# Attention's eight blocks of queries in another order, beside a recurrence

## The reference, cut to what matters

```
for blk in range(S // Q_BLOCK):              # 8 blocks, 8 heads
    q0 = blk * Q_BLOCK; kend = q0 + Q_BLOCK
    s = einsum('bqhd,bkhd->bhqk', q[:, q0:kend], k[:, :kend]) * scale
    s = where(mask, s, -1e30)
    prob = softmax(s)
    outs.append(einsum('bhqk,bkhd->bqhd', prob, v[:, :kend]))
return concatenate(outs).reshape(B, S, 512) @ w_o_mla
...
state = state * d_t + sa[..., None] * b_t + v_t[..., None] * k_t   # per token
y_t   = einsum('bhvk,bhk->bhv', state, r_t)
```

## Time and profile before

| | us |
|---|---|
| median of three runs | 2992.31 |
| the profiled execution | 2994.15 |
| its span, first to last instruction | 2992.1 |
| stage of the attention with the recurrence | 1681 to 1977 |

### The profile page before, as it was taken

The page is one execution under the profiler, slowest core; times in us unless marked ns, Lnnn a source line. Parts: engine busy times, 40 slices in busy tenths (PEclk is TensorE's granted clock), DMA queues, the critical chain, the costliest instruction groups (busy, mean ns, idle before and its releaser), DMA issues.

```text
span 2992.1 us, 37222 instructions
## 1 busy us (share of the span) xinstructions
PE 2851.3 (95%) x15872; PEld 2312.5 (77%) x15872; DVE 1393.9 (47%) x1950; ACT 758.8 (25%) x1027; POOL 362.6 (12%) x286
## 2 busy tenths in 40 slices
PE   5879999999999999999898989889999999999998
PEld 4767878888888888877777667668888888888876
DVE  6994433332323355545544656645343333334454
ACT  4134311111111231124443443332211111111232
POOL 0000201010000101000001602203211110111221
PEclk9999999999999999999999989989999999999999
DMA  3142111111111113334547124343111111111111
GB/s 141 53 82 91 51 57 43 57 42 46 53 42 57 43 46 122 118 137 134 160 152 193 55 58 143 114 148 134 43 43 57 43 57 42 57 43 46 53 57 57
DMA packets 222627, 236.86 MB, mean 79 GB/s; under 512 B 60448, under 2 KB 175008, under 8 KB 221568
## 3 DMA queue, kind: packets, MB, share of 16 engines
q1 hardware_dynamic: 222464, 234.50, 24.5%
HBM read 178.50 MB, written 56.20 MB: 78 GB/s over the span
## 4 chain that ended last, share of the span: by engine, by line
PE 81%; DVE 11%; ACT 3%; issue 2%; SPq 2%; DMA 1%; POOL 1%; DVEq 0%; ACTq 0%; POOLq 0%
PE bank L630 21%; PE bank L632 21%; PE bank L631 21%; PE bank L1812 1%; PE bank L2495 1%; PE bank L1814 1%; PE bank L1813 1%; PE bank L3259 1%; PE bank L3261 1%; PE bank L2750 1%; PE bank L3260 1%; PE bank L3268 1%; DVE stat L2621 1%; DVE w_lo L183 1%; DVE tmp L183 1%
## 5 line engine op out<-in xcount | busy, mean ns | idle before, releaser
L630 PE MATMUL bank<-op_hi,w_hi 128*128 128x512 f32 x1824 | 712.2, 390 | 1.7 <-DVE gates L672 1.5
L632 PE MATMUL bank<-op_hi,w_lo 128*128 128x512 f32 x1824 | 710.5, 390 | 0.0
L631 PE MATMUL bank<-op_lo,w_hi 128*128 128x512 f32 x1824 | 710.4, 389 | 0.0
L630 PEld LDWEIGHTS bank<-op_hi,w_hi 128*128 128x128 f32 x1824 | 343.0, 188 | 74.1 <-issue 2.9
L632 PEld LDWEIGHTS bank<-op_hi,w_lo 128*128 128x128 f32 x1824 | 342.9, 188 | 71.7
L631 PEld LDWEIGHTS bank<-op_lo,w_hi 128*128 128x128 f32 x1824 | 343.0, 188 | 70.9
L183 DVE TENSOR_TENSOR w_lo<-w_raw,w_hi 128x2048 fp32r<-128x2048 f32 (+3 forms) x119 | 256.9, 2159 | 209.3 <-ACT w_hi L432 205.1
L630 PE MATMUL bank<-f_hi,w_hi 128*128 128x512 f32 x864 | 337.4, 391 | 3.2 <-POOL f_lo L183 3.2
L631 PE MATMUL bank<-f_lo,w_hi 128*128 128x512 f32 x864 | 337.3, 390 | 0.0
L632 PE MATMUL bank<-f_hi,w_lo 128*128 128x512 f32 x864 | 337.1, 390 | 0.0
L183 DVE TENSOR_TENSOR hT<-hT,bank 128x512 f32<-128x512 f32 x256 | 169.8, 686 | 316.5 <-PE bank L632 316.2
(11 more groups left out here) (464 smaller groups left out, 3829.9 us busy)
## 6 DMA issues: line engine op xcount, KB each, us to landing
record<-record_scratch SPq DMA_DIRECT2D x16, 1024.0 KB, 5.3
w_raw<-in_w_ffn_up SPq DMA_DIRECT2D x16, 1024.0 KB, 5.1
w_raw<-in_w_ffn_down SPq DMA_DIRECT2D x16, 1024.0 KB, 4.9
w_raw<-in_w_in SPq DMA_DIRECT2D x13, 1024.0 KB, 5.8
w_raw<-in_w_gate SPq DMA_DIRECT2D x11, 1024.0 KB, 5.1
w_raw<-in_w_up SPq DMA_DIRECT2D x11, 1024.0 KB, 5.1
w_raw<-in_w_down SPq DMA_DIRECT2D x10, 1024.0 KB, 4.9
w_raw<-in_w_in SPq DMA_DIRECT2D x17, 512.0 KB, 4.6
```

Of the source, the lines that this page charges most:

```text
L630: t.matmul(ps[:], hi[:, k, wc], x[0][:, k, xc], start=n == 0, stop=False)
L631: t.matmul(ps[:], hi[:, k, wc], x[1][:, (k + turn) % KD, xc], start=False, stop=False)
L632: last = t.matmul(ps[:], lo[:, k, wc], x[0][:, k, xc], start=False, stop=n == kt - 1)
```

## The change

The order of the blocks becomes 6, 5, 4, 1, 2, 3, 0, 7. SPLIT_FIRST becomes 6, so that o is split for the first seven blocks together, which in this order are the columns 0 to 895, in four chunks in steps 60 to 63; w_o's quarters follow in steps 64 to 67; block 7's columns come last, at step 68. The recurrence keeps its steps.

```diff
-    blocks = tuple(reversed(range(SJ)))
+
+    blocks = (6, 5, 4, 1, 2, 3, 0, 7)
     units = [(i, h) for i in blocks for h in range(NH)]
...
-    SPLIT_FIRST = 5
+    SPLIT_FIRST = 6
...
             if done == SPLIT_FIRST and left < 4:
-                split(done, slice(blocks[done] * P, L), left)
+                split(done, slice(0, SPLIT_FIRST * P + P), left)
             elif SPLIT_FIRST < done < SJ and left == 0:
                 split(done, slice(blocks[done] * P, (blocks[done] + 1) * P), slice(0, 4))
             elif done == SPLIT_FIRST and left >= 4:
```

## The result

The changed kernel takes 3003.95 us in the median of seven runs, against 2992.58 for the kernel before in its seven; the ratio is 1.0031, 95% interval 1.0019 to 1.0043, so 9 us slower, between 5.7 and 12.9. The profiled execution took 3006.75 us; its span, 3005.0 us, is 12.9 us longer than that of before. 2.9 us of this lie before the attention's first softmax, in code that did not change (its start is 1689.38 in place of 1686.53), and -0.4 behind the stage; the stage itself, from the first softmax to the first output matmul, is 10.4 us longer.

The account below looks back on a forecast made before the run. TensorE bounds most of the attention stage, its end being loosest; -2.0 - 2.7 - 9.3 + 18.9 + 1.8 = +6.7 us gives a median of 2999.0 us, own range 2994 to 3003, stated range 2988.5 to 3007.

Parts of the forecast that it names:

- rival 2: Block 7 at the end: clock falls to half for 20.3 us, +9 for +1.8, total 3006 us; chance 0.15.
- Solving: Units 0 to 11: VectorE's reduction of scores shrinks 0.13 us in each of 11 units; -2.0 us (-1.0 to -3.2).
- Gap: Units 12 to 16: smaller by 0.44 us each, but the 24.5 us transfer stays, so TensorE waits longer; 0.
- Ends: Units 17 to 21: TensorE-bound, each loses one block of keys; -2.7 us (-1.5 to -3.5).
- Scan: Units 22 to 47: block 1 replaces block 4, less 2.2 us for norms and shorter cover; -9.3 us (-12 to -5).
- The end: Unit 48's softmax to first output matmul: blocks 0 and 7 there take 56.7 us, not 37.8; +18.9 (+11.5 to +24).
- The loop of the split: Units 60 to 62: ScalarE and VectorE alternate on o's split before the next maximum; 5.4 us each, above TensorE's 4.0.
- Clock: Inside block 7 at the end: one short fall, 3.7 us at half clock; +1.8 us (0 to +9).
- The sign that would have made the forecast wrong: Units 48 to 63: clock staying 1.0 there; other signs were an end under 50 us, scan gain under 5 us.
- the rule named beside this term: Trainium skill: many small gaps between matmul groups can make the clock swing repeatedly; units 60 to 63 would not hold full clock.
- The covered end (1): Last eights run at TensorE's pace, drain 8 us, end +11.5; total -7.2, 2985 us; chance 0.16.
- The wash (3): Scan stays covered (-11), solving and ends -5, end +18, no clock fall: +2, 2994.3 us; chance 0.24.

Follow-up runs that it names:

- late halves: Changed kernel, but VectorE does its half of each split one step later, behind the next unit's maximum: ratio 1.0015 against the kernel before.

## Why the prediction was right, and where not

The direction, the size within the stated range of 2988.5 to 3007 and the main steps held: 9 us slower (5.7 to 12.9), against 6.7. That range was wide. By its median the changed kernel, 3003.95 us, lies outside the forecast's own narrower range of 2994 to 3003, and nearer to rival 2's 3006 than to 2999.0; that rival's mechanism, 20 us of half clock inside block 7, did not happen. The stage grew by 10.4 us in the traces: against the terms of the sum the front and the ends gave back 1.4 us less, the scan 0.6 less and the end cost 3.5 more, while the 1.8 for the clock stood for nothing of its own.

- *Solving.* Forecast -2.0. From unit 1 to unit 12 it was -1.8; but the first unit took 0.7 us longer and the transfer's start did not come earlier by as much, so that -0.8 is left at the first "z" matmul. The step was right in kind, its carry to the transfer was too high. How high cannot be read from one pair: this stretch took 81.0 to 82.6 us in five traces that begin with blocks 7, 6, 5 and 80.0 to 82.0 in six that begin with 6, 5, 4.
- *Gap.* Right: the fixed transfer turned 2.6 us of saved work into 2.6 us of wait, 7.1 for 4.5. The kernel with block 7 second shows the converse: work added there costs nothing in the total.
- *Ends.* -2.5 for -2.7, in a pair whose half clock after the wait was equally long (some 20 us). It was so in all six traces that begin with 6, 5, 4, with waits of 6.4 to 7.6 us; in the five that begin with 7, 6, 5, with waits of 4.5 to 5.1 us, it lasted some 20 us three times, and 14 and 7 us in the two others. From the first softmax to unit 22 the means are 112.9 us for the five and 111.4 for the six: the front gave back 1.5 us on the average, not the 3.3 of this pair. Whether the longer wait is what kept the clock low each time was not tested.
- *Scan.* -8.7 for -9.3, but the reasons were mixed up. TensorE's busy time went down by 9.4 us, 127.4 to 118.0, although some 20 us of the scan were at half clock in place of 10: I had charged nothing for the clock here, and 2.2 us for the chain and the norm. With block 3 first the same work gave back 12.3 us (126.5), so that -8.7 came so near to -9.3 was partly luck.
- *The end.* The mis-sized term, +22.4 for +18.9. The loop of the split was right (5.32 us for 5.4), also its reason, by the kernel with late halves. Too low were the units 56 to 59, by 1.2 us (unit 58, 5.2 us: the transposes of block 0's output stand before its scores on TensorE, and wait 1.3 us for VectorE's copy of probT behind two reductions), units 48 to 51 by 0.9 (unit 48 began with 3.4 us of half clock), and the drain, by 2.2: up to 1.5 of that is TensorE at half clock in it (two kernels with late halves and full clock there drain in 12.2 us), which my walk through two queues left out.
- *Clock.* The +1.8 stood at the wrong place. No fall came inside block 7 before its last unit: loops with TensorE idle for a fifth kept full clock. It fell at unit 48, for 3.4 us, in the drain, for 6.8, and in the scan after block 1. The sign that would have made the forecast wrong, a clock of 1.0 in units 48 to 63, was missed only by these two; from unit 49 to unit 62 it was 1.0, also where the rule named beside this term would have had it swing (units 60 to 62). The long fall of the old end, 27 us, is gone with the new order. I did not count that; it is part of why 48 more units of a key block, 21 us by my 0.44, cost no more than 22.4 although the drain alone grew by 8.
- *Rivals.* The covered end (1) asked for an end under 50 us; it was 60, and 53.5 at best with two further edits. Half clock in block 7 for 20 us (2) did not happen. The wash (3) had the end at +18 and the scan at -11; neither.

What the experiments add is the other side of the comparison. The old order's end was poor by the same loop: of its 37.8 us 5.7 to 8.7 went when VectorE no longer waited for ScalarE's half of a split in front of the next maximum, the less when the clock fell all the same. Once this wait is gone on both sides, the descending order wins over the changed one by 0.4%. The reason that remains, from the traces: 48 key-block units leave the front and the scan and come to the end. At the front (22 of them) VectorE, a fixed transfer and the clock after it set the time, and they gave back 3.3 us in this pair, 1.5 on the average; the scan (26) gave back 8.7; at the end all 48 must be paid. How much of the scan's share is the clock alone was not measured by itself: no kernel was run in which the clock was held.

## What to carry to other kernels

Long work belongs where something else sets the time anyway (a fixed transfer, another engine's solve); moved from there to a place that TensorE bounds, it costs its full price (0.38 us for a block of keys of one head here), and at the very end the drain grows with it. Before reordering work to fill an idle tail, ask what the tail waits for: here two engines were handing one chunk back and forth in front of the next unit's first instruction, and putting the second half one step later gained more (0.27%) than any order. When a stretch gets shorter by less work beside a chain, look at the granted clock as well as at the waits, and in more than one trace.

## What the runs showed of the hardware

The fall of the clock in the scan repeats: in all four kernels with block 1 in units 24 to 31 and block 2 behind it the mean granted clock of units 32 and 33 is 0.62 to 0.69 (two of them shown above); in the eight others it is 1.00 in six, and 0.95 (the kernel before) and 0.82 (blocks 1 and 2 changed over, with block 4 in front of these units) in two. In the pair compared above a wait of some 2 us for GpSimd's decay stood before it in both; what differed was how much attention lay around it. And a TensorE busy four fifths of the time, in loops of 5.3 us with waits of 0.9 and 1.2 us in them (units 60 to 62), stayed at full clock for 16 us:

```profile
1960.65:1976.62 15.97, 12.51 (x95) 1.00 0.00 0
```
